# A layer of a streaming encoder in split float32: four places where work is put in another order

## What is computed

```python
z = x @ w_in                                   # GLA q,k,v,r,a; window attention; memory attention; gates
o_a = gla_chunked(...)                         # recurrence over blocks of 64 rows, state 4 x 128 x 128
o_b = windowed attention; o_c = attention to 256 memory rows
mix = (g_a * y_a + g_b * y_b + g_c * y_c) @ w["w_o"]
x = layer_norm(ALPHA * x + mix, ln1_g, ln1_b)
f = conv_ffn(x, ...)   # u = x @ w_up (1024 -> 5632), causal conv of width 3, gelu(gate) * val, @ w_down (2816 -> 1024)
x = layer_norm(ALPHA * x + f, ln2_g, ln2_b)
```

## Time and profile before

| | |
|---|---|
| time, median of 3 runs | 1906.84 us (1902.7 to 1908.04) |
| the profiled execution's own time | 1900.11 us |
| its span | 1898.3 us |
| PE busy | 1840.8 us, 97% of the span |
| DVE / ACT / POOL busy | 52% / 37% / 12% |
| mean granted clock of PE | 0.99 |

### The profile page before, as it was taken

How to read it: one execution, slowest core, us unless ns; L and a number is a source line. 1 busy time by engine, 2 the same in 40 slices (tenths; PEclk the granted TensorE clock), 3 DMA queues, 4 the chain that set the end, 5 groups by cost and what they waited for, 6 DMA issues and landing times.

```text
span 1898.3 us, 31495 instructions
## 1 busy us (share of the span) xinstructions
PE 1840.8 (97%) x12075; PEld 1759.5 (93%) x12075; DVE 984.7 (52%) x1363; ACT 703.7 (37%) x1258; POOL 232.0 (12%) x332
## 2 busy tenths in 40 slices
PE   7999999999899999999999997999999999999997
PEld 7999899999899889998998887999999999999997
DVE  3111144434223355555766478777777776555565
ACT  3221324233222344445334025445444444443432
POOL 0000000000012010000000003323333232001010
PEclk9999999999899999999999999999999999999999
DMA  5111112122131221111446223222222222774753
GB/s 157 45 44 44 45 54 75 56 74 57 51 97 56 78 83 46 41 42 63 142 137 208 82 73 89 80 67 75 82 79 67 89 79 71 263 240 144 229 167 113
DMA packets 180711, 179.59 MB, mean 95 GB/s; under 512 B 20380, under 2 KB 148701, under 8 KB 180636
## 3 DMA queue, kind: packets, MB, share of 16 engines
q1 hardware_dynamic: 178780, 172.56, 29.3%
q0 software_dynamic: 1856, 5.99, 0.9%
HBM read 143.08 MB, written 35.53 MB: 94 GB/s over the span
## 4 chain that ended last, share of the span: by engine, by line
PE 81%; issue 13%; DVE 3%; ACT 1%; DMA 1%; POOL 0%; SPq 0%; ACTq 0%; DVEq 0%; POOLq 0%
PE banks L1390 23%; PE banks L958 14%; PE banks L959 13%; PE banks L960 13%; PE banks L1351 5%; PE banks L1213 3%; PE banks L1182 2%; PE banks L1199 1%; PE banks L1184 1%; DMA w_raw<-in_w_down 1%; DVE w_lo L2450 1%; PE banks L1031 1%; PE banks L1069 1%; PE banks L1073 1%; PE banks L1037 0%
## 5 line engine op out<-in xcount | busy, mean ns | idle before, releaser
L958 PE MATMUL banks<-act_hi,w_hi 128*128 128x352 f32 (+1 forms) x1200 | 401.7, 335 | 4.7 <-DVE w_lo L1984 2.9
L959 PE MATMUL banks<-act_lo,w_hi 128*128 128x352 f32 (+1 forms) x1200 | 391.5, 326 | 0.0
L960 PE MATMUL banks<-act_hi,w_lo 128*128 128x352 f32 (+1 forms) x1200 | 391.3, 326 | 0.0
L1984 DVE TENSOR_TENSOR w_lo<-w_raw,w_hi 128x1024 fp32r<-128x1024 f32 x70 | 86.1, 1231 | 351.1 <-ACT w_hi L1476 351.1
L958 PEld LDWEIGHTS banks<-act_hi,w_hi 128*128 128x128 f32 x1200 | 228.1, 190 | 18.9 <-issue 10.1
L1390 PE MATMUL banks<-x_free_r,a_hi 128*128 128x256 f32 x1232 | 227.6, 282 | 1.8 <-issue 1.0
L959 PEld LDWEIGHTS banks<-act_lo,w_hi 128*128 128x128 f32 x1200 | 228.1, 190 | 1.2
L960 PEld LDWEIGHTS banks<-act_hi,w_lo 128*128 128x128 f32 x1200 | 228.1, 190 | 0.0
L1390 PEld LDWEIGHTS banks<-x_free_r,a_hi 128*128 128x128 f32 x1232 | 190.5, 189 | 2.2 <-issue 2.1
L1390 PE MATMUL banks<-xs_hi,a_hi 128*128 128x274 f32 x616 | 179.6, 292 | 7.7 <-DVE xs_lo L2330 3.1
L1390 PE MATMUL banks<-xs_lo,a_hi 128*128 128x274 f32 x616 | 179.1, 291 | 0.0
(11 more groups left out here) (294 smaller groups left out, 3404.3 us busy)
## 6 DMA issues: line engine op xcount, KB each, us to landing
w_raw<-in_w_down SPq DMA_DIRECT2D x132, 256.0 KB, 3.2
w_raw<-in_w_in SPq DMA_DIRECT2D x100, 256.0 KB, 3.2
gate_in<-gates_scratch SPq DMA_DIRECT2D x24, 529.0 KB, 3.8
h_keep<-conv SPq DMA_DIRECT2D x22, 530.0 KB, 2.7
w_raw<-in_w_up SPq DMA_DIRECT2D x44, 256.0 KB, 3.9
x_free<-in_w_up SPq DMA_DIRECT2D x44, 256.0 KB, 3.5
h_raw<-h_keep SPq DMA_DIRECT2D x22, 384.0 KB, 5.2
gates_scratch<-gate_st SPq DMA_DIRECT2D x32, 176.0 KB, 1.9
```

The lines of the kernel that those rows point to most:

```text
L958: pe.matmul(out, hi, b_hi, start=start, stop=False)
L959: pe.matmul(out, hi, b_lo, start=False, stop=False)
L960: return pe.matmul(out, lo, b_hi, start=False, stop=stop)
L1984: dve.tensor_tensor(dst[:, :, :], w_raw[slot][:, :, :], src[:, :, :].bitcast(F32), ALU.subtract).then_inc(q.w_split_lo, 1)
```

## The change

Five edits in four places, with no arithmetic changed:

1. POOL: `gla_stage` becomes `gla_in` (two copies) and `gla_gate` (silu). For the sample, `gla_in(NT)` stands ahead of the wait for `state_end` and of the two DMAs.
2. PE: the first two w_o tiles are made by turns, chunk by chunk (`wo_first`), then tile 2, then x1(0) and x1(1), then tile 3, and on as before. ACT's order follows.
3. PE, ACT, DVE: half 1 of pair 0 and half 0 of pair 1 are done by turns, one j each; then half 1 of pair 1. The weights of pair 1 are split in the order 0 to 6. ACT and DVE get written-out orders for this and for the window after it.
4. ACT, DVE: the splits of pass 2 of w_down are put ahead of `gelu(LAST)` (ACT) and of the last pair's second `taps` (DVE); DVE's `h_mul(LAST)` moves behind the splits of pass 3.
5. PE, DVE: the first half of the columns of tiles 6 and 7 is turned after pass 58 and gets its statistics in pass 59. The second half is turned, k by k, after the last pass. Tile 7 joins `LN2_POOL`, and tile 7's gain and scale come before tile 8's statistics.

```diff
-    LN2_POOL = (0, 1, 2, 3, 4, 6)
+    LN2_POOL = (0, 1, 2, 3, 4, 6, 7)
...
+        gla_in(NT)
         pool.wait_ge(q.state_end, NT)
         pool.dma_start(O["p_gla"]...)
         pool.dma_start(S_b[:, :, :], I["state_gla"]...)
-        gla_stage(NT)
+        gla_gate(NT)
...
+        def wo_first():
+            pe.wait_ge(q.k_out_ready, 1)
+            pe.wait_ge(q.part_done, 72)
+            for k in WO_USE:
+                pe.wait_ge(q.mix_ready, k + 1)
+                pe.wait_ge(q.w_split_lo, T_WO + WO_ORDER.index(k) + 1)
+                for p in range(2):
+                    last = wo_chunk(p, k)
...
-        wo_tile(0)
-        for p in range(1, 9):
+        wo_first()
+        for p in range(2, 9):
             wo_tile(p)
+            if p == 2:
+                x1(0)
             x1(p - 1)
...
-            if s == 0:
+            if s == 0 or (isinstance(c, int) and c == 1):
                 pe.wait_ge(q.a_lo_done, a_count(c, j))
...
         for j in range(NA):
             block_product(0, 0, 1, j, True)
+            block_product(1, 1, 0, j)
+        for j in range(NA):
+            block_product(1, 1, 1, j)
...
-        pair(1, 1)
...
+            if g == 2 and mh == 1 and k2 == 3:
+                pe.wait_ge(q.out_free, 20)
+                for t in (6, 7):
+                    for k in range(4):
+                        last = late_turn(t, k)
+                    last.then_inc(q.half_turned, 1)
...
-        for t in range(6, 9):
-            r2(t)
+        for k in range(4, KD):
+            pe.wait_ge(q.out_free, 17 + k)
+            for t in (6, 7):
+                last = late_turn(t, k)
+        r2(8)
...
 # ACT, start of the up-projection, after the change
+        c21_out(0, 0, 0)
+        p1_out(0, 0, 1)
+        a_split(1, 1, 0)
+        x_split(1, 2)
+        p1_out(1, 1, 0)
+        p5_out(0, 0, 1)
+        a_split(1, 1, 1)
+        x_split(1, 3)
...
 # ACT, end of the up-projection
         tap(LAST, 1, 1)
+        h_split(*h_of(2))
+        d_split(2)
         gelu(LAST)
...
 # DVE, end of the up-projection
         taps(LAST, 1, 0)
+        h_low(*h_of(2))
+        d_low(2)
         taps(LAST, 1, 1)
-        h_mul(LAST)
-        for q_ in range(2, ND):
+        for q_ in range(3, ND):
             d_low(q_)
             if h_of(q_):
                 h_low(*h_of(q_))
+            if q_ == 3:
+                h_mul(LAST)
```

More of the change, by code:

```diff
@@ L489, in a_count @@
     def a_count(c, j):
-        return FIRST_ORDER.index(j) + 1 if isinstance(c, int) and c == 0 else c * NA + (ORDER.index(j) + 1)
+        if isinstance(c, int) and c < 2:
+            return FIRST_ORDER.index(j) + 1 if c == 0 else NA + j + 1
+        return c * NA + (ORDER.index(j) + 1)
     def raw_count(c, par):
@@ L805, in _, with gla_in @@
     def _(pool):
-        def gla_stage(t):
+        def gla_in(t):
             c, w = tok(t)
@@ L816, in _ @@
         pool.wait_ge(q.proj_free, PS_GATE_A)
-        gla_stage(0)
+        gla_in(0)
+        gla_gate(0)
         with pool.Fori(1, NT) as t:
-            gla_stage(t)
+            gla_in(t)
+            gla_gate(t)
+        gla_in(NT)
         pool.wait_ge(q.state_end, NT)
@@ L1334, in rows_turn, with wo_chunk @@
             last.then_inc(q.rows_turned, 1)
-        def wo_tile(p):
[L1338 to L1344, removed]
-            for k in WO_USE:
[L1346 to L1352, removed]
+        def wo_chunk(p, k):
+            c, b = wo_at(TILES[p]), mix_bank(p)
+            for n_, (x, w) in enumerate(((act_hi, wo_hi), (act_hi, wo_lo), (act_lo, wo_hi))):
+                for half in range(2):
+                    last = pe.matmul(bank(b + half), x[:, k, c:c + P], w[:, k, 512 * half:512 * half + 512],
+                                     start=k == WO_USE[0] and n_ == 0, stop=k == WO_USE[-1] and n_ == 2, skip_group_check=True)
+            return last
+        def wo_first():
[6 more added lines that the diff above has]
+                    last = wo_chunk(p, k)
+                    if k == WO_USE[-1]:
+                        last.then_inc(q.out_mm, 1)
+        def wo_tile(p):
+            pe.wait_ge(q.r_done, p - 1)
+            for k in WO_USE:
+                last = wo_chunk(p, k)
             last.then_inc(q.out_mm, 1)
@@ L1790, in _ @@
         ln_sd_step(0, P, 0)
-        for p in range(1, 8):
+        ln_sd_step(1, P, 1)
+        x1_out(0)
+        for p in range(2, 8):
             x1_out(p - 1)
@@ L2414, in _, with second_window @@
         last.then_inc(q.cleared, 1)
-        for n_ in range(3):
-            combine(0, 0, 1, n_)
-        for j in ORDER[3:]:
-            a_low(1, 1, j)
-        dve.wait_ge(q.cleared, 4)
+        combine(0, 0, 1, 0)
+        combine(1, 1, 0, 0)
+        x_low(1, 5)
+        a_low(1, 1, 4)
+        combine(0, 0, 1, 1)
+        x_low(1, 6)
+        combine(1, 1, 0, 1)
+        a_low(1, 1, 5)
+        combine(0, 0, 1, 2)
+        a_low(1, 1, 6)
+        combine(1, 1, 0, 2)
+        dve.wait_ge(q.cleared, 4)
+        def second_window():
+            taps(0, 0, 0)
+            a_low(2, 0, 0)
+            taps(0, 0, 1)
+            a_low(2, 0, 1)
+            h_mul(0)
+            a_low(2, 0, 2)
+            combine(1, 1, 1, 0)
+            a_low(2, 0, 3)
+            combine(1, 1, 1, 1)
+            a_low(2, 0, 5)
+            a_low(2, 0, 4)
+            combine(1, 1, 1, 2)
+            a_low(2, 0, 6)
         def window(c, par, last=False):
@@ L2521, in _ @@
                     ln2_scale(3 * (g - 1) + (k2 - 5) // 2)
+            if g == 2 and mh == 1 and k2 == 4:
+                for t in (6, 7):
+                    dve.wait_ge(q.half_turned, t - 5)
+                    dve.bn_stats(ln_st[t % 2][:, 0, :], bank(LN2_BANKS[t]))
         for mm in range(4):
             fm_add(5, mm)
-        for t in range(6, 9):
-            ln2_stats(t)
+        for t in (6, 7):
+            dve.wait_ge(q.rows_turned, 9 + t + 1)
+            dve.bn_stats(ln_st[t % 2][:, 1, :], bank(LN2_BANKS[t] + 1)).then_inc(q.stats_done, 1)
+            aggregate(9 + t, t % 2, P)
+        for t in (6, 7):
             ln2_gain(t)
             ln2_scale(t)
+        ln2_stats(8)
+        ln2_gain(8)
+        ln2_scale(8)
 _INS = ("x_prompt", "x_sample", "cache_swa_k", "cache_swa_v", "state_gla", "cache_mem_k", "cache_mem_v", "cache_ffn_conv",
```

69 lines of the change are left out of this document (46 added, 23 removed).

## The result

The changed kernel takes 1915.59 us (median of 5 runs, 1914.96 to 1916.26). The kernel before has a median of 1902.7 over five runs. The ratio is 1.0062, interval 1.0043 to 1.008: slower by 12 us (8 to 15). The forecast was +5.2 us on the profiled execution, 1912.0 in all. The direction and the range hold; the size is less than half of what came, and 1912.0 looks nearer than it is because it starts from a median of three that was 4 us higher.

What follows compares the result with a forecast made beforehand. PE, busy 97% of the span, was taken as the bound, with gains only where it waits or runs at half clock. The terms -8.7 + 1.1 + 11.8 + 2.4 - 1.4 = +5.2 us gave 1912.0, range 1899 to 1925.

Steps and rivals of the forecast that it cites:

- The later steps of the sample ... keep their distances: Sample's recurrence: later steps were not waiting for the two DMAs, so the 8.7 us gain carries through.
- the slow low part beside POOL: Pair turns: DVE's low part takes 1.67 instead of 0.69 beside POOL's sums, +1.5 us (0 to 4).
- pair 2 measured from w_o's end: Up-projection: prediction is wrong as a whole if pair 2 starts less than 7 or more than 16 us later.
- small waits ... 1.3: Pair 1's half 1 after the turns: waits for snapshots and combinations behind the denser DVE queue, 1.3 us.
- Each of the seven turns holds a hand-over: Pair turns: PE idles while ACT and DVE refill the single weight buffer, 1.6 us with the product's end.
- DVE beside POOL's second sum: Tail, last norm: DVE working beside POOL's second 2.33 us sum adds 0.6 us.
- The late store of tile 7: Tail, last norm: tile 7's store goes out just ahead of the sample's, adding 0.6 us.
- 12 to 13 us after the last pass's end: Tail: when the sample's store would appear in the changed profile.
- the first (gaps filled): Half 1 of pair 0: interleaving fills 7.5 us of idleness and removes half clock, -9, time 1891; chance 0.10.
- the third: Pass 4 of w_down: its h block is not late, so early splits gain 4.5 us, time 1905; chance 0.17.
- the fourth: Pair turns: pair 1's weights land earlier, first idleness near 2 us, interleaving costs +6, time 1906; chance 0.13.
- The second: Pair turns: the clock stays low through them, 14 us more, some 3 already counted, time 1923; chance 0.15.

Runs made afterwards that it cites:

- e11: Kernel before with only the sample's earlier gate copies and the last norm's early first-half transposes and statistics: 1893.43 us, ratio 0.9967.
- e12: e11 plus pass 2's early splits, the last h store behind pass 5's transfers, and the wait for its landing moved to pass 7: 1890.43 us, ratio 0.9956.
- e1: Kernel before with only the sample's gate input copied ahead of the wait and the DMAs: 1896.91 us, ratio 0.9967.
- e6: Kernel before with the two pairs by turns, but pair 1's half 0 multiplied with pair 0's weights, so no hand-over: 1909.27 us, ratio 1.0048.
- e9: Kernel before with pairs by turns only after five leading products of pair 0, activation splits ahead of pair 1's weight splits: 1900.36 us, ratio 1.0000.
- e8: Kernel before with pass 2's early splits, and the last h store moved behind the transfers of passes 4 and 5: 1900.54 us, ratio 0.9997.
- e2: Kernel before with only the first two pairs by turns: 1919.31 us, ratio 1.0079.
- e3: Kernel before with only pass 2's splits ahead of the last gelu and the last convolution product behind pass 3's: 1903.95 us, ratio 1.0012.
- e7: Kernel before with the two pairs by turns, half 1 of pair 0 leading by two products: 1927.66 us, ratio 1.0136.
- e5: Kernel before with only the first two w_o tiles by turns, chunk by chunk: 1902.53 us, ratio 1.0009.

## Why the prediction was right in direction and short in size

**Part 1 was right for its own stretch, and in this execution short behind it.** -8.8 for -8.7. The step "The later steps of the sample ... keep their distances" failed here: they ran a stretch at half clock that they had not had, 1.75 by the two traces. It held in e11 and e12, where this distance is 536.2 and 535.8, as in six kernels without part 1 (536.0 to 536.3). Of the 8.8 us, 6.3 (3 to 9) are in the times of e1.

**Part 2 was right**: +1.5 and +1.6 for +1.1, with one wait of 1.21 where the step put it.

**Part 3 was right in mechanism on PE's side and short by 2.8.** The turns came out within 0.3 us, in part since terms cancelled: the slow low part beside POOL cost 0.5 and not 1.5, and a turn at full clock takes 4.7 and not 4.56. By the prediction's own sign, pair 2 measured from w_o's end, it is 14.2 us later (7 to 16 was the bound). The first turn's matmul begins 9.08 us behind half 1's first (1165.7 - 1156.62 = 9.1 forecast), the last turn's 39.2 (39.5 forecast, with the terms for DVE and the clock). The term that failed is the half of pair 1 behind the turns: 10.7 and "small waits ... 1.3" were 13.4 with that last product, and 1208.48 - 1192.34 = 16.1 came. A single wait of 2.35 for a combination, behind two low parts that took 1.7 each beside POOL, and the half clock behind it (3.4 us) make up the 2.7. The kernel before has a wait of the same kind at the end of pair 0's half 1, also with 3.4 us at half clock:

```profile
1174.12 0.56 PE L1390 MATMUL banks<-xs_hi,a_hi 128*128 128x274 f32 x1 [2.43 <-DVE u L2344]
```

The prediction missed it. Its stretch ends at 1174.00, 0.3 us after the clock fell, and so shows 0.99; and its "many small" idle times are six, of which two, 2.17 and 2.43, are more than half. Alone the part costs 15.0 by the times. The step "Each of the seven turns holds a hand-over" is true but is not all of the cause. The hand-overs account for what e6 took away, 10.7 of 17.8 us by the traces and 6 of 15 by the medians; the share is not known better than that. The rest, 7 to 9 us, goes with the first weight split, waiting for its transfer ahead of the activation splits in ACT's and DVE's queues, with the order that follows from it. I had that wait as PE's, for weights; e6 shows that it is the queues' too, and would be there if PE wanted no weights at all. e9, in which neither the order nor the hand-over is on PE's path, has no loss; it changes both at once, and so shows that the two together are the cause, not which weighs more.

**Part 4 was right in mechanism.** The wait is at pass 4, 5.58 (4.9 forecast) and 5.2 alone, behind the late store; +3.9 alone by the distance for +2.4. Counted from the last combine the store is issued 4.1 us later than before (4.4 forecast). e8 shows the store as the cause, and a link that the step didn't see: SP's wait for the store's landing.

**Part 5 was right in sum, in part by luck**: the tail is 2.3 shorter (2.35 forecast), the transposes cost 1.04. Inside it two terms were off against each other. DVE beside POOL's second sum was put at 0.6, and its last step took 2.61 in place of 1.27, so 1.3. The late store of tile 7 was put at 0.6, and the time from the sample's store to the end grew by 0.2. The sign "12 to 13 us after the last pass's end" was wrong: it is 11.0, and the sum itself would have given 10.5 to 11.1.

**Left over.** Of the 9.5 us between +5.2 and +14.7 of the profiled spans, 2.8 are part 3's, 1.75 the stretch behind part 1, 0.8 part 4's up to pass 6, 0.4 part 2's. 1.8 lie later in w_down, in waits for `w_lo` that are 1.6 longer than before; the prediction had no term for them. Part 4 alone has them as long (4.9 for 3.3), but e6, without part 4, waits 2.4 us at a place where the kernel before waits for nothing, so no run ties them to a part. 2.0 lie ahead of tile 7, where nothing was changed; the changed kernel's profile had half-clock stretches at 12 to 18 and 32 to 35 us, and most of the experiments had none, and part 4 with its store moved (e8) had two in the same place. They seem to be of the execution, and the times, +12, hold less of them than the spans.

Of the rivals, the first (gaps filled) is refuted by the changed kernel and by e2, the third by the 5.58 us wait and e3, the fourth by the 7.28 us wait. The second was wrong for this kernel and right for e7. The chances, added as the prediction describes and with nothing of rivals 3 and 4 on slower, give slower 0.375 and same 0.485; it states 0.42 and 0.44.

## What to carry to other kernels

Before one puts the work of a second block between that of a first, one asks for each in-order queue what its new first instruction waits for. A copy that waits for a transfer, put ahead of copies whose data is there, stops both blocks, even where the matrix engine has no use for its result yet. And a store that is issued later is priced by all that stands behind it in its queue: the transfers, and the wait for its landing.

## What the runs showed of the hardware that I had not expected

- The clock fell to 0.57 and 0.58 over 4 us in the middle of work for which the trace has no idle time of PE (13.00 of 13 and 9.00 of 9 us busy ahead), just behind the 24 small matmuls named above, in two of the four kernels with part 1. In e11 and e12, which have part 1 and the same small matmuls, it stayed at 1.00.
- The same code at the same place ran a half-clock stretch in one execution and none in another. Behind the 2.6 us wait at pass 2 the clock was 0.76 over 7 us in e11 and 1.00 in e5, and from the sample's gate to w_o, which no part touches, the distance was 531.5 in the kernel before and 536.0 in part 5 alone, whose clock was 0.79 over 880 to 896 where the kernel before had 1.00. Nine of the fourteen profiles have the same three stretches of 3.4 us at half clock there; the kernel before, the changed one and e9 have none of them. A single pair of traces can't tell a change of 2 us in such a stretch; a milestone taken over many kernels can.
- A subtraction of VectorE of 128x512 took 0.69 us alone and 1.20, 1.73 and 1.77 beside POOL's sums. It is not slowed evenly. Each of these three began while a sum of POOL ran, and ended 0.55 us after that sum had ended, whenever it had begun: 1160.93 + 1.20 = 1162.13 against 1160.32 + 1.27 = 1161.59. In the fourteen profiles 870 `a_lo` subtractions began with over 0.15 us of a sum of POOL left, and every one ended 0.5 to 0.6 us after that sum. So the price is what is left of POOL's instruction when VectorE's starts, less 0.14 us (0.69 - 0.55).
